# Second-tile ranks of the context dealt among its first tile's expert rows, and the context's experts dealt at three rates

## The chip, the cores and the metric

The kernel runs on one core of a Trainium2 chip. The metric is the device time of one execution in microseconds (us), the median of the runs shown. The program is one fixed order of instructions for each engine: PE (TensorE), DVE (VectorE), ACT (ScalarE), POOL (GpSimd) and SP (SyncE, which issues the loads of the weights). Engines wait for each other on semaphores alone.

## The reference, cut to what matters

256 tokens of width 1024, all in fp32, pass through a first model of two layers (a retention and state-space mixer, then a SwiGLU) and then through a second model of two layers (attention with a Fourier and a pooling branch, then a PEER layer that looks up 128 experts for each token). The second model also has a context of 256 tokens of its own, which nothing of the first model feeds: its modulation, its mixer and its PEER layer can be computed beside the first model.

```python
def _peer(h, w_pq, peer_keys, peer_down, peer_up):
    q = (h @ w_pq).reshape(B, L, PEER_HEADS, 2, PEER_QDIM // 2)
    s = jnp.einsum("blhpd,hpkd->blhpk", q, peer_keys)
    sv, si = lax.top_k(s, PEER_TOPK)                       # two top-16 of 128 for each of 8 heads
    cand = (sv[..., 0, :, None] + sv[..., 1, None, :])     # 256 sums
    top_s, pos = lax.top_k(cand, PEER_TOPK)                # the best 16, their experts' indices
    gate = jax.nn.softmax(top_s, axis=-1)
    a = jnp.einsum("tkd,td->tk", peer_down[ee], hh)        # one gathered row per expert
    act = gg * jax.nn.gelu(a)
    return jnp.einsum("tk,tkd->td", act, peer_up[ee])      # and a second one
```

## The kernel before, in words

A class `Plan` first writes one list of items (`put`), and five functions then turn the list into the engines' instructions, so an engine's order is the order of the items. Two generators write the items. The **main stream** (`x_stream`) is the first model and then the second model's two layers for the 256 tokens. The **context stream** (`context_stream`) is everything of the context. `streams` deals between them: each step of a generator says what it costs (`yield 7`; a step without a number costs 7), and the context is given its next step while its sum is at most the main stream's sum times a pace. The context changes the pace itself at three points: `PACES` is 0.8 in its modulation, 1.8 in its mixer, 1.1 in its queries and ranks, and 0.72 in its experts. When the first model is over (`yield "alone"`), what is left of the context is put at once; here the context ends a few items before that.

The first model's layer is, in this order: `conv_in` chunks, four groups of heads (`heads`, `group_gate`, `group_stats`, `group_turn`), a merge (`branch_gate`, `branch_out`), four retention heads, a second merge, the output product (`mix_out`, four products), a normalisation (`row_stats`, `row_turn`), 22 `ffn_in` products, 8 `ffn_out` and 2 `ffn_last`. Nearly every product is 32 PE records of one 1 MB weight chunk, about 7 us. After an `ffn_in` product DVE does two operations (L1966, L1968) that free the PSUM bank; four banks rotate, and `ffn_out` waits for the last L1968. In a group of heads PE waits for L1896, the decay factors that DVE makes.

The context's PEER layer is `peer_c`. For each of two tiles of 128 tokens and each of 8 heads a rank is made on DVE: `rank_keys` twice (L2130 to L2138, top 16 of 128), `rank_pairs` (L2149 and L2130 to L2138, top 16 of 256) and `rank_index` (L2157 to L2183, the experts' numbers). In the kernel before, `route` puts all 16 ranks, both tiles', before the first expert row. Then come 512 steps in the order (tile 0: 128 downs, 128 ups; tile 1: 128 downs, 128 ups), 1.5 of cost each. A step reads one row of 4 KB per partition, 0.52 MB in all, which POOL fetches by index (`fetch`, L2556) into a ring of nine places; a **down** (L2234) multiplies the row with the token's vector and sums, an **up** (L2245) adds the row times its activation to the result. A fetch of place i waits for the step that read the place before (`rows_read`), and the first nine wait for `gates_ok[1, 0]`, the gates of the second tile:

```python
rr = Ring([Slot(ar.get(1024), self.sem(f"row{i}")) for i in range(gslots)])
...
put("fetch", ..., before=s.before or gates_ok[1, 0])
```

The nine places lie where the queries, the keys and the scores were. `peer_add` closes the context: it loads a row into the first place and adds the result to the context. The main stream needs the context only in the second model.

Two merges, one in each layer, read DVE's L1954 and L1957; `mix_out` waits for the last of them.

## Time and profile before

| | before |
| --- | --- |
| median of 3 runs | 4141.52 us (4139.63 to 4145.15) |
| span of the profiled execution | 4145.5 us |
| PE busy | 3651.7 us, 88% |
| DVE busy | 2321.9 us, 56% |
| POOL busy | 1280.9 us, 31% |
| rows fetched by index | 855.71 MB, 51.5% of the 16 DMA engines' span |
| weights and the rest on SP's queue | 350.32 MB, 22.2% |

The profiled execution has no time of its own beside its span; the span lies within the range of the runs, 4.0 us above their median, and all sums are made against it. The first model fills about the first 2177 us, the second model the other 1969. "Busy" of PE counts the modelled time of its matmuls. The granted clock (PEclk) is a share of full speed; idle time is given before the group of instructions that ends it, with what it had waited for.

### The profile page before, as it was taken

The page shows a single profiled execution, that of the slowest core. Times are in us where ns is not written, and L with a number is a line of the kernel's source. Part 1 is how long each engine was busy: PE and PEld are TensorE (multiplying, and loading weights), DVE is VectorE, ACT ScalarE, POOL GpSimd, SP SyncE. Part 2 cuts the span into 40 slices and gives each one's busy share as a digit, 9 for nine tenths or more (in the row PEclk, how much of TensorE's full clock was granted, in tenths as well). Part 3 has the DMA queues.
Part 4 walks back from the last instruction along what each step waited for, and adds up shares of the span by engine and source line. Part 5 has one row for each costly group of instructions (what it writes and reads, how often), then busy time and mean ns, then how long its engine had stood idle before and what let it go on. Part 6 is the DMA issues. An engine that isn't in the chain of part 4 may idle for free. (4 is left out here: it accounts for less than half of the span.)

```text
span 4145.5 us, 41044 instructions
## 1 busy us (share of the span) xinstructions
PE 3651.7 (88%) x14584; PEld 2584.5 (62%) x14584; DVE 2321.9 (56%) x5464; ACT 657.1 (16%) x1800; POOL 1280.9 (31%) x1125
## 2 busy tenths in 40 slices
PE   8988999999989889999988989778788898877777
PEld 6666788887756778888846875333335686433332
DVE  3432011457676897775762137787763226777875
ACT  2332101110001230000002211111112211111111
POOL 1100000000664566664540003445441002444442
PEclk9999999999999899999999999999999999998899
DMA  8742344334998889998973349999996227999997
GB/s 324 283 194 88 117 151 180 134 111 145 369 411 292 295 330 395 405 389 340 413 298 125 108 152 384 415 416 401 419 415 256 103 107 288 404 420 420 418 420 331
DMA packets 207818, 1208.65 MB, mean 292 GB/s; under 512 B 23696, under 2 KB 24848, under 8 KB 96000
## 3 DMA queue, kind: packets, MB, share of 16 engines
q0 software_dynamic: 154368, 855.71, 51.5%
q1 hardware_dynamic: 53248, 350.32, 22.2%
q8 instruction: 118, 1.93, 0.2%
q14 instruction: 84, 0.69, 0.0%
HBM read 1204.79 MB, written 1.15 MB: 291 GB/s over the span
## 5 line engine op out<-in xcount | busy, mean ns | idle before, releaser
L1363 PE MATMUL bank<-big 128*128 128x256 f32 (+5 forms) x9848 | 2148.4, 378 | 59.5 <-issue 8.7
L1363 PEld LDWEIGHTS bank<-big 128*128 128x128 f32 (+2 forms) x9848 | 1839.0, 192 | 374.3 <-issue 67.4
L2556 POOL DMA_INDIRECT big<-in_pboth,big x1024 | 1217.5, 1189 | 1210.0 <-PE bank L1750 695.2
L1750 PE MATMUL bank<-big 128*128 128x512 f32 x2048 | 984.3, 638 | 251.2 <-ACT big L2520 251.0
L2234 DVE CUSTOM_DVE_ANT_0 big<-big 128x1024 f32<-128x1024 f32 x768 | 928.0, 1224 | 347.1 <-DMA big<-in_pboth,big 343.0
L1750 PEld LDWEIGHTS bank<-big 128*128 128x128 f32 x2048 | 407.5, 204 | 816.6 <-issue 481.4
L2543 POOL TENSOR_TENSOR big<-big 128x1 f32<-128x1 f32 (+1 forms) x49 | 37.4, 763 | 1499.4 <-DVE big L1804 1499.4
L2245 DVE SCALAR_TENSOR_TENSOR big<-big 128x1024 f32<-128x1024 f32 x254 | 326.2, 1284 | 61.3 <-DMA big<-in_pboth,big 41.5
L2520 ACT ACTIVATE big<-big 128x128 f32<-128x128 f32 x512 | 165.1, 391 | 254.9 <-DVE big L2213 248.2
L1398 PE MATMUL bank<-big 128*128 128x128 f32 x596 | 93.0, 290 | 63.5 <-ACT big L2365 20.1
L2510 ACT ACTIVATE big<-big 128x4 f32<-128x4 f32 (+2 forms) x134 | 27.7, 207 | 742.3 <-DVE big L2209 742.2
L1553 PE MATMUL bank<-big 128*128 128x512 f32 x256 | 114.5, 609 | 23.4 <-DVE big L1968 23.4
L2090 DVE TENSOR_REDUCE big<-bank 128x1 f32<-128x512 f32 (+1 forms) x48 | 28.9, 602 | 175.0 <-PE bank L1651 174.1
L1398 PEld LDWEIGHTS bank<-big 128*128 128x128 f32 x596 | 72.9, 151 | 80.8 <-issue 35.2
L1877 DVE SCALAR_TENSOR_TENSOR big<-big,bank 128x512 f32<-128x512 f32 x32 | 22.0, 687 | 148.8 <-ACT big L2346 148.8
L1553 PEld LDWEIGHTS bank<-big 128*128 128x128 f32 x256 | 49.8, 195 | 87.2 <-issue 63.1
L1954 DVE SCALAR_TENSOR_TENSOR big<-big,bank 128x256 f32<-128x256 f32 x32 | 13.4, 420 | 153.4 <-PE bank L1363 153.3
L1861 DVE SCALAR_TENSOR_TENSOR big<-bank,big 128x255 f32<-128x255 f32 (+1 forms) x144 | 62.7, 477 | 60.0 <-ACT big L2334 58.3
L2303 ACT ACTIVATE big<-big 128x1024 f32<-128x1024 f32 x26 | 27.4, 1056 | 428.4 <-DVE big L1974 170.8
L2112 DVE SCALAR_TENSOR_TENSOR big<-big,bank 128x512 f32<-128x512 f32 x36 | 24.8, 688 | 103.6 <-PE bank L1363 103.6
L2488 ACT ACTIVATE big<-bank,big 128x256 f32<-128x256 f32 x72 | 30.3, 472 | 282.1 <-PE bank L1363 282.1
L2549 POOL DMA_DIRECT2D big<-in_wmod x48 | 25.9, 542 | 150.9 <-PE bank L1575 150.9
(203 smaller groups left out, 2177.4 us busy)
## 6 DMA issues: line engine op xcount, KB each, us to landing
big<-in_w SPq DMA_DIRECT2D x104, 1024.0 KB, 7.7
big<-in_wmod POOLq DMA_DIRECT2D x48, 1024.0 KB, 9.0
big<-in_wgu SPq DMA_DIRECT2D x44, 1024.0 KB, 8.1
big<-in_wzg SPq DMA_DIRECT2D x36, 1024.0 KB, 4.8
big<-in_wro SPq DMA_DIRECT2D x32, 1024.0 KB, 6.9
big<-in_wpq SPq DMA_DIRECT2D x24, 1024.0 KB, 6.0
big<-in_wd SPq DMA_DIRECT2D x22, 1024.0 KB, 8.4
big<-in_pboth,big POOLq DMA_INDIRECT x1024, 11.7
```

What stands on the lines that cost most here:

```text
L1363: last = pe.matmul(o, a, b, start=(i == 0), stop=(i == n - 1))
L1398: last = pe.transpose(o[:, i, :], b, ident)
L1553: last = pe.matmul(us[2 * tt + n].ap, act[:, 2 * i + k, tt * P:tt * P + P], wk[:, k, 512 * n:512 * n + 512], start=(i + k == 0), stop=False)
L1750: last = pe.matmul(u.ap, d.ap, row[:, 512 * i:512 * i + 512], start=(k == 0), stop=(k == 127))
L1861: i = v.scalar_tensor_tensor(c[:, m, s:256], o[:, m, 0:256 - s], conv["w"][m][:, 3 - s:4 - s], c[:, m, s:256], ALU.mult, ALU.add)
L2090: step(v.reduce_max(sm[:, c:c + 1], u.ap[:, 0:nk * P], AX.X))
L2234: v.tensor_tensor_reduce(row, row, h, 1.0, 0.0, ALU.mult, ALU.add, out).then_inc(done[0], 1)
L2245: v.scalar_tensor_tensor(at, s.ap, by, at, ALU.mult, ALU.add).then_inc(done[0], 1)
L2488: last = e.activation(sc.ap[:, m, :], by2(u.ap)[:, m, :], ACT.Tanh, scale=0.5, bias=bias[m])
L2520: s.activation(d.ap, p.ident, ACT.Copy, scale=by).then_inc(diag[0], 1)
L2543: g.tensor_tensor(r.sm[:, 8 + r.at:8 + r.at + r.n], r.sm[:, 4 + r.at:4 + r.at + r.n], r.sm[:, 12:13].to_broadcast([P, r.n]), ALU.pow).then ...
L2556: g.indirect_dma_start(out=s.ap, out_offset=None, in_=table, in_offset=bass.IndirectOffsetOnAxis(ap=index, axis=0)).then_inc(s.full[0], 16)
```

## The change

Five things change, all in how the context is dealt.

1. `ranks` can be asked for one tile. `route` puts the first tile's 8 ranks only; the second tile's come one step at a time (`rank_keys`, `rank_keys`, `rank_pairs`, `rank_index`) before every third down of the first tile, steps 2, 5, 8 and so on to 101. The cost of those steps counts in the dealing as before.
2. The first downs therefore start when the first tile's gates are there (`gates_ok[0, 0]`).
3. The scores of the second tile and the scratch of the ranks must outlive the first downs. They move to the end of the context's memory (`kept`, 3248 columns), so only six places for rows fit at first; three more are placed at step 102, behind the second tile's gates (`gates_ok[1, 0]`). Places are no ring any more but a list of free ones, taken in the order in which they came free.
4. The pace of the experts is 0.9 instead of 0.72 until the main stream enters its second layer, 0.55 from there to that layer's first merge, and 0.75 after it. The main stream sets these two (`PACES[4]`, `PACES[5]`).
5. `peer_add` takes the first free place.

No operation is added or removed, on no engine: 32 `rank_keys`, 16 `rank_pairs`, 16 `rank_index`, 256 downs, 256 ups and 512 fetches in both. The items of the main stream keep their order. From line 1050 on lines are numbered up to 24 higher in the changed kernel; the down is L2258 there, the up L2269, the fetch L2580, L1954 and L1957 are L1978 and L1981.

```diff
--- before.py
+++ after.py
@@ -126,7 +126,7 @@
         self.before, self.ss, self.var, self.done = before, ss, var, done
 
 
-PACES = (0.8, 1.8, 1.1, 0.72)
+PACES = (0.8, 1.8, 1.1, 0.9, 0.55, 0.75)
 A_SIZE = 27648
 BIG_N = 53208
 SIDE = 8300
@@ -338,6 +338,8 @@
             yield 1.5
 
         for l in range(2):
+            if l:
+                yield "pace", PACES[4]
             blk = [0]
 
             def chunk(blk=blk, l=l):
@@ -571,6 +573,8 @@
                         yield 7.2 if first or n < 6 else 1
                     s.free(u.free)
 
+            if l:
+                yield "pace", PACES[5]
             yield from merge(True, y_ok, group_end(3, gots[3]))
             yield from head_qk(0, gots[4])
             for h in range(3):
@@ -1042,11 +1046,12 @@
         else:
             self.x_ok = done
 
-    def routing(self, ar, b2, wr, sm, l, vec, hT, hT_ok, keys, keys_ok, iot, iot_ok, tvs, gat, eix, qts, GH):
+    def routing(self, ar, b2, wr, sm, l, vec, hT, hT_ok, keys, keys_ok, iot, iot_ok, tvs, gat, eix, qts, GH, kept=None):
 
 
         put, tick, t = self.put, self.tick, self.t
         SC0 = Ring([Slot(ar.get(256, (2, 128))) for _ in range(3 if GH == 8 else 8)])
+        ar = kept or ar
         SC1 = ar.get(2048, (8, 256))
         rk = dict(cand=ar.get(256, (16, 16)), oh=ar.get(512, (32, 16)), sv=ar.get(32, (2, 16)), si=ar.get(32, (2, 16)),
                   sf=ar.get(32, (2, 16)), tp=ar.get(16).bitcast(U32), ab=ar.get(32, (2, 16)), ia=ar.get(32, (2, 16)),
@@ -1098,8 +1103,8 @@
             scores.append((sc, v.free))
             ended["keys"] = v.full
 
-        def ranks(asking=None):
-            for tt in range(2):
+        def ranks(asking=None, tiles=(0, 1)):
+            for tt in tiles:
                 for h in range(8):
                     while asking and len(scores) <= h:
                         next(asking)
@@ -1109,14 +1114,14 @@
                         yield from gates(tt, h // GH)
 
         def route():
-            first = rank_all = ranks()
+            first = ranks(tiles=(0,))
             for i in range(9):
                 if i < 8:
                     query(i)
                     yield 7
                     score(i)
                 for _ in range(4 if i else 0):
-                    yield next(rank_all)
+                    yield next(first)
             yield from first
 
         return route, query, score, ranks, ix_ok, gates_ok, ended
@@ -1146,32 +1151,51 @@
         got = yield from self.peer_queries(banks, sm, start, size, l, X, 1, self.c_ok, 2)
         ar, mark, h2, act, gat, eix, gl, hT, hT_ok, keys, rest = got
         m3 = ar.at
+        kept = Arena(self.big, start + size - 3248, 3248)
         rows = self.modulated_rows(l, 1, 3, "norm2", h2, [ar.get(1024) for _ in range(3)], self.b_free)
         rows_ok = yield from rows(hT_ok)
         ar.at = m3
         qts = Ring([Slot(ar.get(512, (2, 256)))])
         qts.slots[0].freed = rows_ok
-        tvs = [ar.get(128, (8, 16)) for _ in range(2)]
-        route, _, _, _, ix_ok, gates_ok, _ = self.routing(ar, banks, wr, sm, l, 1, hT, hT_ok, tvs=tvs, gat=gat, eix=eix, qts=qts,
-                                                       GH=8, **rest)
+        tvs = [kept.get(128, (8, 16)) for _ in range(2)]
+        route, _, _, ranks, ix_ok, gates_ok, _ = self.routing(ar, banks, wr, sm, l, 1, hT, hT_ok, tvs=tvs, gat=gat, eix=eix,
+                                                              qts=qts, GH=8, kept=kept, **rest)
         yield from route()
         yield "pace", PACES[3]
+        assert ar.at <= size - 3248
         ar.at = mark
-        rr = Ring([Slot(ar.get(1024), self.sem(f"row{i}")) for i in range(gslots)])
+        free = []
+
+        def place(ready):
+            s = Slot(ar.get(1024), self.sem(f"row{len(free) + len(ahead)}"))
+            s.freed = ready
+            free.append(s)
+
+        second = ranks(tiles=(1,))
         steps = [(kind, tt, k) for tt in range(2) for kind in range(2) for k in range(128)]
         pending, ahead, nxt, act_ok = [], [], 0, {}
         acc_ok = {}
+        while ar.at + 1024 <= size - 3248:
+            place(gates_ok[0, 0])
         for n, (kind, tt, k) in enumerate(steps):
-            while nxt < len(steps) and len(ahead) < gslots:
+            if n < 102 and n % 3 == 2:
+                yield next(second)
+            if n == 102:
+                assert next(second, None) is None
+                while len(free) + len(ahead) < gslots:
+                    place(gates_ok[1, 0])
+            while nxt < len(steps) and free:
                 kind2, tt2, k2 = steps[nxt]
-                s = rr.take()
+                slot = free.pop(0)
+                s = Turn(slot)
                 put("fetch", table=t["pboth"].rearrange("e (a d) -> (e a) d", a=2), s=s, index=eix[kind2][:, tt2, k2:k2 + 1],
-                    ready=ix_ok[tt2][k2 // 16] if k2 % 16 == 0 else None, before=s.before or gates_ok[1, 0])
-                ahead.append(s)
+                    ready=ix_ok[tt2][k2 // 16] if k2 % 16 == 0 else None, before=s.before)
+                ahead.append((s, slot))
                 nxt += 1
-            s = ahead.pop(0)
+            s, slot = ahead.pop(0)
             done = tick("rows_read")
             s.free(done)
+            free.append(slot)
             if kind == 0:
                 put("down", row=s.ap, full=s.full, h=h2[:, tt, :], out=act[:, tt, k:k + 1], done=done)
                 if k == 127:
@@ -1185,7 +1209,7 @@
                 acc_ok[tt] = done
             yield 1.5
         end = tick("peer_added")
-        put("peer_add", m5=rr.slots[0].ap, src=self.mods[l, 1, 5:6, :].to_broadcast([P, 1024]), loaded=tick("d_m5_c", 16),
+        put("peer_add", m5=free[0].ap, src=self.mods[l, 1, 5:6, :].to_broadcast([P, 1024]), loaded=tick("d_m5_c", 16),
             before=[done], acc=h2, X=X, done=end)
         self.c_ok, self.b_free = end, [end]
```

How DVE's order moves, at two places.

The end of the first layer's second merge, DVE, between two pairs L1954, L1957 of the merge (in the changed kernel L1978, L1981). Before, a pair and the first ten of the 29 rows that follow it up to the next pair:

```order
L1954 SCALAR_TENSOR_TENSOR big<-big,bank 128x256
L1957 TENSOR_TENSOR big<-big 128x256
L2130 MAX big<-big 128x8
L2132 MAX_INDEX big<-big 128x8
L2134 MATCH_REPLACE big<-big 128x128
L2136 MAX big<-big 128x8
L2138 MAX_INDEX big<-big 128x8
L2130 MAX big<-big 128x8
L2132 MAX_INDEX big<-big 128x8
L2134 MATCH_REPLACE big<-big 128x128
L2136 MAX big<-big 128x8
L2138 MAX_INDEX big<-big 128x8
```

The same place in the changed kernel:

```order
L1978 SCALAR_TENSOR_TENSOR big<-big,bank 128x256
L1981 TENSOR_TENSOR big<-big 128x256
L2258 ISA big<-big 128x1024
L2258 ISA big 128x1
L2173 TENSOR_TENSOR big<-big 128x256
L2154 MAX big<-big 128x8
L2156 MAX_INDEX big<-big 128x8
L2158 MATCH_REPLACE big<-big 128x256
L2160 MAX big<-big 128x8
L2162 MAX_INDEX big<-big 128x8
L2258 ISA big<-big 128x1024
L2258 ISA big 128x1
```

Before, a whole rank (two `rank_keys`, shown, then a `rank_pairs` and a `rank_index`) stands in this one gap. Now all that stands there is shown: two downs (an L2258 pair each) and one `rank_pairs`.

The second layer's groups of heads, DVE, one stretch from a group's mask (L1887) to the next group's first decay factor (L1895, L1896), where L2245 is the up. Before:

```order
L1887 TENSOR_TENSOR big<-bank,big 128x128
L2245 SCALAR_TENSOR_TENSOR big<-big 128x1024 x3
L1877 SCALAR_TENSOR_TENSOR big<-big,bank 128x2x256
L2245 SCALAR_TENSOR_TENSOR big<-big 128x1024 x2
L1906 TENSOR_TENSOR big<-big 128x512
L1908 TENSOR_TENSOR big<-big,bank 128x512
L1910 TENSOR_TENSOR big<-big 128x512
L1906 TENSOR_TENSOR big<-big 128x512
L1908 TENSOR_TENSOR big<-big,bank 128x512
L1910 TENSOR_TENSOR big<-big 128x512
L2245 SCALAR_TENSOR_TENSOR big<-big 128x1024 x2
L1895 SCALAR_TENSOR_TENSOR big<-big 128x256
```

In the changed kernel:

```order
L1911 TENSOR_TENSOR big<-bank,big 128x128
L2269 SCALAR_TENSOR_TENSOR big<-big 128x1024 x2
L1901 SCALAR_TENSOR_TENSOR big<-big,bank 128x2x256
L2269 SCALAR_TENSOR_TENSOR big<-big 128x1024 x3
L1930 TENSOR_TENSOR big<-big 128x512
L1932 TENSOR_TENSOR big<-big,bank 128x512
L1934 TENSOR_TENSOR big<-big 128x512
L1930 TENSOR_TENSOR big<-big 128x512
L1932 TENSOR_TENSOR big<-big,bank 128x512
L1934 TENSOR_TENSOR big<-big 128x512
L1919 SCALAR_TENSOR_TENSOR big<-big 128x256
```

Seven ups stood in this stretch and five do now; none is left in front of the next group's first decay factor.

The counts of context items by stretch of the main stream, as the two orders have them, are these; the prediction uses them.

| stretch of the main stream | before | changed |
| --- | --- | --- |
| between the last five products of the first layer's second merge | 6 keys, 3 pairs, 4 index | 10 downs, 2 keys, 1 pairs, 1 index |
| then to the last `row_turn` | 4 keys, 2 pairs, 1 index | 8 downs, 2 keys |
| then to the 22nd `ffn_in` | 71 downs, 4 keys, 2 pairs, 3 index | 65 downs, 10 keys, 6 pairs, 6 index |
| then to the second layer's first `row_turn` | 35 downs | 35 downs, 2 keys, 1 pairs, 1 index |
| then to the second layer's `dt_sums` (8 input products) | 22 downs, 15 ups | 9 downs, 23 ups |
| then to the last of its four groups of heads | 86 ups | 66 ups |
| then to the end of its second merge | 35 ups, 128 downs | 41 ups, 128 downs |
| then to the last `row_turn` | 7 ups | 8 ups |
| then to the 22nd `ffn_in` of the second layer | 84 ups | 87 ups |

## Rows read from the trace of the kernel before

**Rows 1.** The page's first line.
```profile
span 4145.5 us, 41044 instructions
```
**Rows 2.** Busy time by stretch; the first of them gives the columns.
```profile
core 0: us, PE busy (x) PEld busy (x) DVE busy (x) ACT busy (x) POOL busy (x), PEclk, DMA share, GB/s
...
1017.00:1194.00 177.00, 155.43 (x705) 134.71 (x706) 128.60 (x283) 8.57 (x23) 98.03 (x80) 0.95 0.90 354
...
1280.00:1361.00 81.00, 67.61 (x306) 58.01 (x306) 71.41 (x134) 12.55 (x27) 45.64 (x36) 0.90 0.87 313
1361.00:1567.00 206.00, 174.49 (x924) 154.32 (x924) 178.69 (x252) 67.86 (x191) 118.67 (x92) 0.92 0.85 315
1600.00:1896.00 296.00, 291.36 (x1333) 248.27 (x1332) 204.54 (x356) 19.59 (x43) 193.14 (x149) 0.99 1.01 399
1935.00:2099.00 164.00, 152.93 (x705) 133.21 (x705) 123.06 (x129) 8.47 (x22) 100.06 (x84) 0.98 0.99 397
...
2177.00:4146.00 1969.00, 1638.73 (x5237) 953.68 (x5235) 1136.37 (x3138) 351.22 (x1034) 582.82 (x529) 0.94 0.78 316
```
**Rows 3.** PE in order of time, end of the first layer's merge: start, length, idle before.
```profile
965.93 7.20 PE L1363 MATMUL bank<-big 128*128 128x256 f32 x32 [2.01 <-DVE big L1954]
978.50 30.09 PE L1363 MATMUL bank<-big 128*128 128x256 f32 x128 [5.37 <-issue]
...
1017.74 14.57 PE L1363 MATMUL bank<-big 128*128 128x256 f32 x66 [0.94 <-DVE big L1812]
```
**Rows 4.** PE in order of time, first layer's SwiGLU.
```profile
1054.28 126.83 PE L1363 MATMUL bank<-big 128*128 128x256 f32 x576 [8.54 <-DVE big L1968]
1193.40 21.79 PE L1553 MATMUL bank<-big 128*128 128x512 f32 x45 [12.29 <-DVE big L1968]
```
**Rows 5.** DVE in order of time, the context's last rank and its first down.
```profile
1031.89 0.30 DVE L2130 MAX8 big<-big 128x8 f32<-128x128 f32 x1
...
1033.74 0.29 DVE L2130 MAX8 big<-big 128x8 f32<-128x128 f32 x1
...
1042.37 0.29 DVE L2188 TENSOR_TENSOR big<-big 128x128 f32<-128x128 f32 x1
...
1052.20 1.23 DVE L2234 CUSTOM_DVE_ANT_0 big<-big 128x1024 f32<-128x1024 f32 x1 [8.10 <-DMA big<-in_pboth,big]
```
**Rows 6.** DVE by line, 1055 to 1194: count, busy us, mean ns, idle before.
```profile
L2234 DVE CUSTOM_DVE_ANT_0 big<-big 128x1024 f32<-128x1024 f32 x71 | 86.5, 1225 | 37.0 <-DMA big<-in_pboth,big 35.8
L1968 DVE TENSOR_TENSOR big<-big,bank 128x256 f32<-128x256 f32 x21 | 8.9, 422 | 0.7
```
**Rows 7.** The fetches L2556 from issue to landing, 1080 to 1190, saturated.
```profile
DMA to landing us min/median/max: 11.8/16.0/18.1
```
**Rows 8.** The same, 1350 to 1500.
```profile
DMA to landing us min/median/max: 4.9/6.5/9.7
```
**Rows 9.** POOL's time for one fetch, 1080 to 1190 and 2560 to 2700.
```profile
L2556 POOL DMA_INDIRECT big<-in_pboth,big x56: 935/974/1893, 1079.3 to 1189.1; - x56
...
L2556 POOL DMA_INDIRECT big<-in_pboth,big x55: 935/941/1791, 2560.6 to 2697.3; - x55
```
**Rows 10.** PE by line, second layer's groups of heads, 1361 to 1567.
```profile
L1484 PE MATMUL bank<-big 128*128 128x128 f32 x128 | 20.6, 311 | 6.0 <-DVE big L1849 6.0
...
L1474 PE MATMUL bank<-big 128*128 128x64 f32 x64 | 12.5, 279 | 13.0 <-DVE big L1896 13.0
L1398 PE MATMUL bank<-big 128*128 128x128 f32 x48 | 8.3, 301 | 14.6 <-ACT big L2365 14.6
```
**Rows 11.** DVE by line, the same stretch: the ups.
```profile
L2245 DVE SCALAR_TENSOR_TENSOR big<-big 128x1024 f32<-128x1024 f32 x89 | 114.3, 1284 | 7.7 <-issue 0.4
```
**Rows 12.** DVE by line, 1935 to 2099, second layer's SwiGLU: the ups.
```profile
L2245 DVE SCALAR_TENSOR_TENSOR big<-big 128x1024 f32<-128x1024 f32 x85 | 109.2, 1285 | 40.2 <-DMA big<-in_pboth,big 36.7
```
**Rows 13.** PE in order of time, the wait that ends that stretch.
```profile
2098.87 57.02 PE L1553 MATMUL bank<-big 128*128 128x512 f32 x128 [11.07 <-DVE big L1968]
```

## The prediction

> **What bounds the kernel now.** I start from the span [rows 1] and cut it by stage with the table of busy time [rows 2]. The last 1969 us are the second model; no item of it moves, so only the first 2177 us can change. There PE is what is waited for: nearly each product of 7 us follows the one before, and the time is PE's work plus the gaps in which it waits. So the question is which gaps the context's items cause, and I read PE in order of time for them. At the end of the first layer's merge there are gaps of 2.01 and 5.37 us [rows 3]: DVE is working off whole ranks, 10.5 us each (from the first MAX8 at 1031.89 to the gates at 1042.37) [rows 5], dealt at one per product of 7 us. In the first SwiGLU there are 8.54 and 12.29 us [rows 4]. The first of them is a chain: DVE finishes the last rank, only then may the first row be fetched, the down at the head of DVE's queue waits 8.10 us for it [rows 5], and PE's L1968 is behind that down. The second gap is DMA: from 1055 on the downs idle 37.0 us, 35.8 of them for their rows [rows 6]. In the second layer's groups of heads it is DVE itself: 178.7 of 206 us busy, PE only 174.5 [rows 2], with gaps of 13.0 us behind the decay factors, 14.6 behind ACT and 6.0 behind the step sizes [rows 10], while 89 ups take 114.3 us of DVE [rows 11]. The last gap is 11.07 us, before the second layer's `ffn_out` [rows 13]: again the ups idle 40.2 us, 36.7 of them for rows [rows 12], at a DMA share of 0.99 [rows 2].
>
> A gap also costs PE speed. The four output products behind the 5.37 us gap take 30.09 us for 128 records, 0.235 us each; behind the 8.54 us gap 576 records take 126.83 us, 0.220 each [rows 3, 4]. 128 × 0.015 is 1.9 us lost to the lower granted clock, which stands at 0.95 in the SwiGLU, at 0.92 in the heads and at 0.99 in the stretch with hardly a gap [rows 2].
>
> **Term 1, the merge of the first layer.** Between its last five products DVE had 6 keys, 3 pairs and 4 index steps. A key step is 1.85 us (1031.89 to 1033.74), a whole rank 10.5 [rows 5], so this is some 34 us over some 28 us of PE. Now it is 10 downs and one step of each other kind. A down is 1.225 us [rows 6] and the read of its sum behind it, 1.28 from start to start: 10 × 1.28 + 10.5 = 23 us. DVE keeps up, and of 2.01 + 5.37 us there is left what the last pair of operations needs, under 2. With the 1.9 us of clock the gain is **8 us**. What could take the place: the first row is asked for when the first gates are done and holds DVE up, by at most the 8.1 us of [rows 5]; but that is four products earlier, and 28 − 23 us of slack and a bank's depth lie between.
>
> **Term 2, the first SwiGLU.** The last `row_turn` now ends at 1017.7 − 8 = 1009.7 [rows 3]. From there to the 22nd L1968 DVE has 65 downs (65 × 1.28 = 83.2), six ranks less two key steps (6 × 10.5 − 2 × 1.85 = 59.3) and 22 pairs of 0.42 us [rows 6] with a handover (22 × 0.86 = 18.9), in all 161.4 us. PE needs 22 × 32 × 0.220 = 155. So DVE, not DMA, sets this stage now. To it I add waits for rows. The bounds are 0 and the 37.0 us of [rows 6]. Six places instead of nine speak for more, but the rows needed fall from 71 to 65 over a stretch that saturated DMA with 71, and steps of ranks between the downs give the fetches time. Fetches below saturation land in 6.5 us, in saturation in 16.0 [rows 7, 8]; with issue and down a place turns round in 6.5 + 2.2 = 9 us at best, and six of them are wanted each 6 × 161/65 = 15 us. I take 4 us, near the good end. `ffn_out` then starts at 1009.7 + 161.4 + 4 = 1175 instead of 1193.4: **18 us with term 1**. PE still waits some 10 us there, now for DVE.
>
> The Trainium skill speaks against this very interleaving. First the row: a fetch takes POOL 974 ns at the median where only downs run, and 941 ns in a stretch of the second model in which ranks run beside the fetches, each with four casts and five scalar operations [rows 9]. By the page "SBUF — State Buffer", section "Who interferes with whom", a copy, cast or tensor_scalar in a two-port mode shuts GpSimd out of their shared port pair, and with it the writing of descriptors for DMAs issued by POOL. By that rule each rank could add up to the length of its casts to a fetch; by the row it adds nothing, and the sum goes by the row.
>
> **Term 3, `ffn_out` to the second layer's `dt_sums`.** 35 downs stand in `ffn_out` and `ffn_last` in both, four rank steps (10.5 us) come on top, in a stage where PE asks DVE for nothing: hidden, if DVE is not behind by more than its last 20 us. Then 22 downs and 15 ups (22 × 1.28 + 15 × 1.3 = 48 us) become 9 and 23 (41 us). PE idles 81 − 67.6 = 13 us here [rows 2], for DVE. But nine of the downs stand in front of the very first input product. **5 us** gain, between 0 and 8.
>
> **Term 4, the heads.** 86 ups become 66: 20 × 1.3 = 26 us of DVE go (1.284 each [rows 11]). Of the 33.6 us of gaps [rows 10] the 6.0 is behind a queue that gets one up shorter, the 13.0 is behind ups put in front of the decay factors, the 14.6 behind ACT, which waits for DVE further up. DVE falls to 153 of 206 us, PE's 174 then lead. Bounds: 0, if the chain DVE, ACT, PE in a group costs the same however short the queue; 26, all of DVE's relief; 33.6 and some clock is a limit it cannot pass. I take a bit over half: **15 us**.
>
> **Term 5, what was put off.** At the end of the heads 12 experts are missing from the count (20 fewer ups there, 8 more before). They come back where DMA is saturated: 6 more rows in the second merge stage (share 1.01, 399 GB/s [rows 2]) one behind it and 3 more in the second SwiGLU (0.99); the last two come after that. A row of 0.524 MB is 1.31 us at 399 GB/s. In the first of these PE idles only 296 − 291.4 = 4.6 us, with nine rows in hand; of 6 × 1.31 = 8 us of DMA I let 2 through. In the second the wait for DMA is already open [rows 13], and all of 3 × 1.31 = 4 adds to the 11.07. **6 us loss**, between 1 and 12. `peer_add` moves behind the main stream's first `ffn_add`, where DVE waits for PE; nothing. Queue order on POOL: the roots of the normalisations now have fetches before them in the first layer too; each fetch waits for an earlier down only, so at most one issue of 0.94 us each, nothing.
>
> **The sum:** −18 − 5 − 15 + 6 = −32 us against a span of 4145.5, so 4113. The median of the runs lies 4.0 below the profiled span: 4141.5 − 32 = 4109.5, I say **4109**.
>
> **The rivals.**
> - *Heads give nearly everything, and more clock.* Terms 3 and 4 at their good ends, 8 + 26, no waits in term 2 (4) and 3 in term 5: some −50, **4091**. For it: PE loses speed behind each gap. Against: a group's own chain stays. 0.15.
> - *The put-off rows come back in full.* Term 5 at 12, and term 4 at 6, because ACT's share of the gaps stays: −18 − 5 − 6 + 12 = −17, **4124**. For it: share 1.01 in the stage that gets more. 0.17.
> - *The dealing moves the gaps without closing them*, so the change doesn't do what it says: DVE-bound first SwiGLU with 15 more us of waits, heads at 6, term 5 at 12: about **4139**. 0.10.
> - *Six places are too few: slower.* Place: the downs up to step 102, in the first SwiGLU. If fetches land there as in saturation, 16.0 to 18.1 us [rows 7], a place turns in about 18 to 20 us, a row comes each 3.0 to 3.4 us, and the 65 rows need 195 to 220 us instead of 161, that is 34 to 59 us of waits instead of 4. It is slower than before from 36 us on, a turn of some 18.2 us; between 36 and 59 us, at 48, the total is **4153**. For it: the ring shrinks by a third while the pace rises. Against: fewer rows ask DMA for less, and landing falls as soon as it is not saturated [rows 8]. 0.08.
>
> **How the numbers follow.** The forecast has 0.50 (its own range 4096 to 4122), the rivals 0.15, 0.17, 0.10 and 0.08. The range leaves out the fast rival's outer half, most of the slow one and half of the unmoved one: 4086 to 4138. Within 0.2% (8.3 us, about what a measurement of this kernel can tell from none) is 4133.2 to 4149.8. Faster by more: 0.50 + 0.15 + 0.17 less a bit for the tails, 0.80; same 0.12; slower 0.08.
>
> **What would show it.** Right: the first down at about 940, no wait of 8 us at DVE for it; the gap before `mix_out` under 2 us; no gap at the fifth `ffn_in`; a gap of about 10 us before the first `ffn_out`, at about 1175, with DVE busy over 0.9 in that stage and its DMA share under 0.9; the gaps of the heads near half of 33.6; the gap before the second `ffn_out` at about 15. Wrong: downs that idle more than 15 us for rows in the first SwiGLU (the six places), heads with gaps above 28 us (a chain, no queue), or gaps for rows in the second merge stage, where there are none now.

## The result, and the profile after

| | before | changed |
| --- | --- | --- |
| median | 4143.34 us (4 runs) | 4096.9 us (4 runs, 4094.54 to 4104.84) |
| ratio of the runs, changed to before | | 0.9894, 95% interval 0.9882 to 0.9906 |
| span of the profiled execution | 4145.5 us | 4095.9 us |

The change makes the kernel 1.06% faster, 46 us between the medians, where 32 were forecast. In a later comparison on another occasion it came to 0.9891 (0.9875 to 0.9908).

The busy time by stretch in the changed kernel, columns as in [rows 2], each stretch cut at the same products of the main stream as there:

```profile
1006.00:1162.00 156.00, 153.53 (x706) 133.53 (x707) 145.95 (x389) 8.45 (x22) 76.88 (x65) 1.00 0.94 359
...
1246.00:1321.00 75.00, 64.92 (x306) 55.33 (x306) 66.16 (x116) 12.31 (x27) 40.59 (x31) 0.95 0.85 306
1321.00:1511.00 190.00, 170.01 (x925) 150.20 (x926) 154.26 (x233) 68.65 (x193) 95.77 (x73) 0.96 0.80 287
1544.00:1842.00 298.00, 290.07 (x1325) 246.96 (x1324) 213.75 (x362) 19.55 (x42) 197.03 (x155) 0.99 1.01 404
1880.00:2051.00 171.00, 153.38 (x705) 133.56 (x706) 129.03 (x134) 8.45 (x22) 113.80 (x87) 0.96 0.99 397
...
2129.00:4096.00 1967.00, 1644.83 (x5236) 954.81 (x5234) 1135.04 (x3137) 350.83 (x1034) 580.68 (x529) 0.94 0.78 316
```

The first SwiGLU went from 177 to 156 us, the input products and heads from 81 + 206 to 75 + 190, and the second SwiGLU from 164 to 171. The table below has the same from the start of one product of the main stream to the start of another; the last two columns compare it with the terms of the prediction.

| stretch of the main stream | before | changed | difference | forecast |
| --- | --- | --- | --- | --- |
| start to the first layer's fourth retention head, 882 (order unchanged) | 881.9 | 877.9 | −4.0 | 0 |
| to the first `ffn_in` (term 1) | 135.8 | 128.9 | −6.9 | −8 |
| to the first `ffn_out` (term 2) | 175.7 | 154.5 | −21.2 | −10 |
| to `dt_sums` (term 3) | 160.5 | 154.7 | −5.8 | −5 |
| to the second layer's first merge product (term 4) | 224.5 | 204.5 | −20.0 | −15 |
| to its first `ffn_in` (term 5) | 356.6 | 360.3 | +3.7 | +2 |
| to its first `ffn_out` (term 5) | 163.9 | 169.6 | +5.7 | +4 |
| to the end | 2046.6 | 2045.5 | −1.1 | 0 |

PE in order of time, at the places of [rows 3, 4] and [rows 13]:

```profile
968.01 27.97 PE L1387 MATMUL bank<-big 128*128 128x256 f32 x128 [1.12 <-issue]
...
1161.27 19.16 PE L1577 MATMUL bank<-big 128*128 128x512 f32 x44 [1.64 <-DVE big L1992]
...
2050.43 9.80 PE L1577 MATMUL bank<-big 128*128 128x512 f32 x18 [16.81 <-DVE big L1992]
```

The 5.37 us before `mix_out` are 1.12, and the four products behind it take 27.97 us instead of 30.09: that is the clock, granted at 1.00 over these four products where it was 0.93 before, with the lower level at their start, behind the gap. The gap of 8.54 us is gone, that of 12.29 is 1.64, and the last one grew from 11.07 to 16.81. DVE by line in the first SwiGLU, against [rows 6], and the fetches' landing there:

```profile
L2258 DVE CUSTOM_DVE_ANT_0 big<-big 128x1024 f32<-128x1024 f32 x66 | 77.9, 1217 | 0.1
L1992 DVE TENSOR_TENSOR big<-big,bank 128x256 f32<-128x256 f32 x22 | 9.3, 422 | 0.8
L1990 DVE SCALAR_TENSOR_TENSOR big<-big,bank 128x256 f32<-128x256 f32 x22 | 9.2, 418 | 5.1 <-ACT big L2429 5.0
```
```profile
DMA to landing us min/median/max: 5.0/8.6/10.4
```

The downs idle 0.1 us instead of 37.0; DVE even waits 5 us for ACT. The rows land in 8.6 us instead of 16.0 [rows 7], with ranks between the downs and with six places instead of nine; how much of it the places alone do is seen below, in the run with six places throughout. The price I had wrong is in the same kernel, DVE in order of time:

```profile
1010.67 1.21 DVE L2258 CUSTOM_DVE_ANT_0 big<-big 128x1024 f32<-128x1024 f32 x1
1011.80 0.08 DVE L2258 DVE_READ_ACCUMULATOR2_ANT big<- 128x1 f32 x1
1011.80 1.22 DVE L2258 CUSTOM_DVE_ANT_0 big<-big 128x1024 f32<-128x1024 f32 x1
```

From one down to the next it is 1.13 us, not 1.28. In the kernel before, every pair of downs at 1.28 us has a wait for the row in it, 0.04 or 0.05 us in the trace, and the few pairs without such a wait follow each other at 1.14 to 1.15 there too.

The heads, PE by line, against [rows 10]:

```profile
L1508 PE MATMUL bank<-big 128*128 128x128 f32 x128 | 18.7, 292 | 3.8 <-DVE big L1873 3.8
...
L1498 PE MATMUL bank<-big 128*128 128x64 f32 x64 | 12.0, 269 | 5.0 <-DVE big L1920 5.0
L1422 PE MATMUL bank<-big 128*128 128x128 f32 x49 | 8.6, 300 | 14.7 <-ACT big L2389 11.8 <-ACT big L2344 2.9
```

33.6 us of gaps are 23.5, of which 2.9 belong to a turn that stands outside the stretch of [rows 10]. 13.0 behind the decay factors became 5.0. PE's own time in these stretches fell as well, from 174.5 to 170.0 us, at a granted clock of 0.96 instead of 0.92.

### The profile page after: what moved, and what is told of

The parts are those of the page before. It is cut to its first block and busy times, and to the rows that moved or that the text cites. A ratio compares the mean times of both kernels' runs of the same rounds, so it can differ in the third digit from the quotient of the medians.

```text
span 4095.9 us, 41049 instructions
## 1 busy us (share of the span) xinstructions
PE 3641.8 (89%) x14584; PEld 2573.2 (63%) x14584; DVE 2316.0 (57%) x5464; ACT 656.3 (16%) x1800; POOL 1283.3 (31%) x1125
## 3 DMA queue, kind: packets, MB, share of 16 engines
HBM read 1204.79 MB, written 1.15 MB: 294 GB/s over the span
## 5 line engine op out<-in xcount | busy, mean ns | idle before, releaser
L2580 POOL DMA_INDIRECT big<-in_pboth,big x1024 | 1217.8, 1189 | 1277.7 <-PE bank L1774 700.4
L2258 DVE CUSTOM_DVE_ANT_0 big<-big 128x1024 f32<-128x1024 f32 x768 | 926.0, 1222 | 317.7 <-DMA big<-in_pboth,big 314.0
L2269 DVE SCALAR_TENSOR_TENSOR big<-big 128x1024 f32<-128x1024 f32 x254 | 326.2, 1284 | 65.8 <-DMA big<-in_pboth,big 45.4
L1978 DVE SCALAR_TENSOR_TENSOR big<-big,bank 128x256 f32<-128x256 f32 x32 | 13.5, 421 | 147.8 <-PE bank L1387 147.8
L2327 ACT ACTIVATE big<-big 128x1024 f32<-128x1024 f32 x26 | 27.4, 1055 | 363.7 <-DVE big L1998 128.2
```

What stands on the lines that cost most here:

```text
L2258: v.tensor_tensor_reduce(row, row, h, 1.0, 0.0, ALU.mult, ALU.add, out).then_inc(done[0], 1)
L2269: v.scalar_tensor_tensor(at, s.ap, by, at, ALU.mult, ALU.add).then_inc(done[0], 1)
L2580: g.indirect_dma_start(out=s.ap, out_offset=None, in_=table, in_offset=bass.IndirectOffsetOnAxis(ap=index, axis=0)).then_inc(s.full[0], 16)
```

## The experiments

Theory A is that of the prediction: the order of the ranks closes the first layer's gaps, the low pace those of the heads, and rows put off are paid for where DMA is saturated. All are made from the changed kernel, except where it is said, and all twelve keep the main stream's order. Stage times are from the profiled executions, in the table's sense.

### The order alone, the paces alone

```diff
-PACES = (0.8, 1.8, 1.1, 0.9, 0.55, 0.75)
+PACES = (0.8, 1.8, 1.1, 0.72, 0.72, 0.72)
```

> The changed kernel with its experts at 0.72 throughout, so only the order of the second tile's ranks and the six and then nine places are new. Theory A (the order closes the first layer's gaps, the low pace the heads' gaps, and what is put off costs about 9 us): the first layer keeps nearly all of its 32 us, the heads' 18 and the input products' 8 are lost, the 9 us of put-off rows are not paid: about 4115 us, gap before the second ffn_out near 11 us. Theory B (the three paces do it, the order only permits them): the gap before the first ffn_out is 8 us or more again and the total 4130 or above.

Measured: 4140.42 us, ratio 0.9998 (0.9987 to 1.0008). Neither number was met, but the stages tell why. The first layer keeps its gain: 154.6 us from its first `ffn_in` to the first `ffn_out`, where the changed kernel has 154.5, with a gap of 1.76 us. The heads take 222.8 us again (86 ups), the second SwiGLU 163.2. What had not been in the expectation is the end. The rank steps now cost their share of 0.72 beside the rows, so ten rows are left when the first model is over; they are put at once, and the second model's first product waits. PE in order of time:

```profile
2181.53 1.94 PE L1422 MATMUL bank<-big 128*128 128x128 f32 x8 [28.57 <-DVE big L2061]
```

So the order is worth its 28 us in the first layer at the old and at the new paces, and at the old pace the second model gives 27 back, because the context isn't finished.

The kernel before with the new paces (its list of ranks and its ring as they were):

```diff
-PACES = (0.8, 1.8, 1.1, 0.72)
+PACES = (0.8, 1.8, 1.1, 0.9, 0.55, 0.75)
...
+            if l:
+                yield "pace", PACES[4]
...
+            if l:
+                yield "pace", PACES[5]
```

> The kernel before, all ranks ahead of the first row and nine places at once, with the three new paces (0.9, 0.55, 0.75). Theory A: the first row's wait of 8 us stays, and at 0.9 the downs ask for 4.2 rows and a weight chunk in each 7 us, above what DMA gave (414 GB/s), so the gap before the first ffn_out grows to 20 us or more; the heads gain some 18, the end loses a few: 4135 to 4150 us. Theory B (the paces do it): 4110 or less.

Measured: 4158.79 us, ratio 1.0032 (1.0021 to 1.0044): the paces without the order are slower than the kernel before. The first SwiGLU takes 197.5 us (36.8 + 160.7) instead of 175.7; the heads take 203.1, as with the new order. DVE by line and the stretch itself, 1052 to 1211:

```profile
L2238 DVE CUSTOM_DVE_ANT_0 big<-big 128x1024 f32<-128x1024 f32 x87 | 104.8, 1224 | 39.0 <-DMA big<-in_pboth,big 38.2
```
```profile
1052.00:1211.00 159.00, 130.37 (x575) 110.79 (x573) 119.28 (x216) 7.34 (x19) 109.04 (x89) 0.93 1.02 409
```

89 rows at 409 GB/s: DMA is full. What the order gives the first SwiGLU is therefore that 59 us of DVE work on ranks lies there and takes the place of rows, beside the row that no longer has to be waited for. That the rows are fewer (65 instead of 89) is counted; how the gain divides between the two is not.

### The heads: how much an up costs

```diff
-PACES = (0.8, 1.8, 1.1, 0.9, 0.55, 0.75)
+PACES = (0.8, 1.8, 1.1, 0.9, 0.75, 0.75)
```

> The changed kernel with 0.75 instead of 0.55 in the second layer's heads. Theory A (gaps in the heads are DVE's queue of ups): the heads take 18 to 22 us longer, the context ends earlier, and the gap before the second ffn_out is no longer than 17 us: about 4112. Theory C (the gaps there are the chain DVE, ACT, PE of a group and the gain came from the clock and the input products): under 8 us longer, about 4100.

Measured: 4140.65 us, ratio 0.9997 (0.9987 to 1.0007). More than I expected: this one number gives back nearly all the change had won. 26.5 us are the heads (231.0 with 90 ups against 204.5 with 66) and 8.6 the input products (78.2 against 69.6; 40 rows against 32); from the second merge to the SwiGLU it is 6.9 us more, the SwiGLU itself 3.4 more. The SwiGLU's part has another cause: the context ends inside it, the gap before `ffn_out` is only 2.00 us, and one product before it PE waits for a weight chunk instead. The section on moving rows shows why. PE in order of time:

```profile
2085.12 9.88 PE L1387 MATMUL bank<-big 128*128 128x256 f32 x32 [15.23 <-DMA big<-in_wgu]
```

PE by line in the heads:

```profile
L1508 PE MATMUL bank<-big 128*128 128x128 f32 x128 | 21.5, 320 | 6.6 <-DVE big L1873 6.6
...
L1498 PE MATMUL bank<-big 128*128 128x64 f32 x64 | 13.3, 292 | 14.7 <-DVE big L1920 14.7
L1422 PE MATMUL bank<-big 128*128 128x128 f32 x48 | 8.4, 302 | 13.2 <-ACT big L2389 13.2
```

The ends of the gaps are the same engines as in the changed kernel; what changed with the number of ups is how long they last, and the time of a matmul (320 ns against 292 in the first row): the clock stood at 0.90 there and at 0.96 in the changed kernel. What an up costs here is therefore DVE's time and the clock together.

```diff
-PACES = (0.8, 1.8, 1.1, 0.9, 0.55, 0.75)
+PACES = (0.8, 1.8, 1.1, 0.9, 0.35, 0.75)
```

> The changed kernel with 0.35 in the second layer's heads: 42 ups instead of 66 in the groups of heads and 23 instead of 32 rows in the input products; 23 rows are left for the end of the first model. From the runs so far an up in the heads costs about 1.0 us (86, 66 ups: 224.5, 204.5 us from dt_sums to the second merge's first branch_out). Theory A (DVE's queue all the way): about 182 us. Theory C (a group's own chain takes over once the queue is short): 195 us or more. The rows left over cost at least 30 us at the start of the second model, so the total is 4105 to 4130 either way.

Measured: 4125.32 us, ratio 0.9962 (0.9948 to 0.9976). From `dt_sums` to the merge 184.8 us with 42 ups. The points are 231.0, 204.5 and 184.8 us at 90, 66 and 42 ups, with 222.8 at 86 in the changed order at the old pace and 224.5 at 86 in the kernel before: 0.9 to 1.0 us for an up between 86 and 66, some 2 above 86, 0.8 below 66. Theory A holds nearly all the way, and the chain begins to show; PE by line:

```profile
L1508 PE MATMUL bank<-big 128*128 128x128 f32 x128 | 17.8, 282 | 0.4 <-DVE big L1873 0.4
...
L1498 PE MATMUL bank<-big 128*128 128x64 f32 x64 | 11.5, 261 | 0.0
L1422 PE MATMUL bank<-big 128*128 128x128 f32 x60 | 10.1, 296 | 10.2 <-ACT big L2389 8.7 <-ACT big L2344 1.5
```

Nothing is left behind the decay factors; 8.7 us behind ACT are still there. Whether fewer ups would shorten those too was not run. The total is lost at the end, where 23 rows were left over, and one wait is 46.99 us:

```profile
2160.54 1.94 PE L1422 MATMUL bank<-big 128*128 128x128 f32 x8 [46.99 <-DVE big L2061]
```

### The end: rows left over

```diff
-PACES = (0.8, 1.8, 1.1, 0.9, 0.55, 0.75)
+PACES = (0.8, 1.8, 1.1, 0.9, 0.55, 0.72)
```

> The changed kernel with 0.72 instead of 0.75 from the second layer's first merge on; some nine rows are left for the end of the first model and are put there at once. Theory A (the put-off rows cost DMA time in the saturated stage, one row 1.3 us): the gap before the second ffn_out falls from 16.8 to 11 to 13 us, total 4090 to 4096, if the rows at the end hide beside ffn_last and the first products of the second model. Rival: the rows at the end hold the second model's first rows up by 9 x 1.3 us, total 4100 or more.

Measured: 4104.17 us, ratio 0.9904 (0.9888 to 0.9921). The total is the rival's, and both mechanisms are there: the gap before the second `ffn_out` is 9.69 us, shorter than theory A's 11 to 13 (83 rows instead of 87, the stage 7.1 us shorter), and 17.31 us of gap stand at the start of the second model. Only two rows were left by the order, not nine; but ups put off stood before them, and `peer_add` behind them. DVE in order of time, the last of the context and the main stream's next operation:

```profile
2127.84 9.80 DVE L2269 SCALAR_TENSOR_TENSOR big<-big 128x1024 f32<-128x1024 f32 x7
2142.11 2.36 DVE L2288 TENSOR_TENSOR big<-big 128x1024 f32<-128x1024 f32 x2 [4.46 <-DMA big<-mods]
2144.50 2.36 DVE L2291 TENSOR_TENSOR big<-big 128x1024 f32<-128x1024 f32 x2
...
2147.72 0.75 DVE L2061 TENSOR_SCALAR big<-big 128x1024 f32<-128x1024 f32 x1 [0.67 <-POOL big L2567]
```

Seven ups (9.8 us), a load that is asked for only when the last up is done (4.5) and the four operations of `peer_add` (4.7) stand in DVE's queue before L2061. Whether one row or ten is left, this tail is paid: 17 us for two, 29 for ten, 47 for 23, that is 1.4 us for each further row, which is what an up takes behind another. The paces of the changed kernel end the context one product before the end of the first model, and pay none of it. The prediction had no term for this tail.

### The places

```diff
-        while ar.at + 1024 <= size - 3248:
+        while len(free) < 4:
             place(gates_ok[0, 0])
```

> The changed kernel with four places for rows instead of six until step 102 (then nine, as before). Theory A (in the first SwiGLU DVE's own work sets the stage, a place turns round in landing 8.6 us and 2.2 us more, 11 us, and is wanted again after as many rows as there are places, 2.4 us each): four places give one row per 2.7 us, some 0.3 us too slow, so the stage from the first ffn_in to the first ffn_out grows by 10 to 20 us from 154.5 and the total is 4105 to 4117. Rival (places have slack, landing shortens with the load): under 3 us longer, total below 4100.

Measured: 4127.13 us, ratio 0.9961 (0.9947 to 0.9976). The total is above the expected 4105 to 4117. The first SwiGLU takes 173.2 us instead of 154.5 (+18.7), within the 10 to 20 expected; the downs idle 20.5 us for rows although these land in 7.1:

```profile
L2258 DVE CUSTOM_DVE_ANT_0 big<-big 128x1024 f32<-128x1024 f32 x55 | 66.0, 1220 | 20.5 <-DMA big<-in_pboth,big 20.4
```

Another 6 us are lost before it, from the fourth retention head to the first `ffn_in` (135.0 against 128.9): the gap before `mix_out` is 5.29 us again. With six places the list has slack, with four it is what the stage waits for.

```diff
-        yield from self.peer_c(self.pb, Ring(few), self.smallb, self.B0 + mark, BIG_N - self.B0 - mark, 9, 0, self.C)
+        yield from self.peer_c(self.pb, Ring(few), self.smallb, self.B0 + mark, BIG_N - self.B0 - mark, 6, 0, self.C)
```

> The changed kernel with six places for rows to the end instead of nine from step 102 on. Theory A (places matter only while they turn round slower than rows are wanted; in saturation landing was 16 us with nine places because nine stood in DMA's queue, and with six it shortens): the saturated stages of the second layer take at most 10 us longer, total 4097 to 4107. Rival (landing stays at 16 us, a place turns in 18, six give a row per 3 us where one per 2.1 is wanted): the second SwiGLU alone grows by 40 us or more, total 4140 or above.

Measured: 4125.0 us, ratio 0.9959 (0.9944 to 0.9973), 26 us behind the changed kernel on the same occasion (4098.74): between the two expectations. The mechanism is A's, the size is not. In the second SwiGLU the fetches land in 9.5 us instead of 15.9:

```profile
DMA to landing us min/median/max: 4.8/9.5/12.6
```

so a place does turn faster when fewer are in the queue, and that stage loses 3.0 us. But in the stages before it 5.1 us go in the input products, 2.2 + 8.3 in the second merge and retention heads and 5.6 in its end, 4.4 of them in the gap before `mix_out`. In the merge stage DVE idles 69.8 us for rows, where it is 15.3 in the changed kernel; DVE by line, 1525 to 1870:

```profile
L2258 DVE CUSTOM_DVE_ANT_0 big<-big 128x1024 f32<-128x1024 f32 x128 | 154.5, 1226 | 61.3 <-DMA big<-in_pboth,big 60.5
L2269 DVE SCALAR_TENSOR_TENSOR big<-big 128x1024 f32<-128x1024 f32 x32 | 41.1, 1285 | 11.9 <-DMA big<-in_pboth,big 9.3 <-DVE big L2269 0.5
```

Nine rows in hand bridge most of that. The three places that come back at step 102 are worth 22 us in the profiled executions, about as much as the relief of the heads.

### Can rows be moved out of the saturated stage?

Two kernels put other paces into the second layer's `ffn_in` and `ffn_out`: 0.68 and 0.95, and 0.66 and 1.05.

```diff
-PACES = (0.8, 1.8, 1.1, 0.9, 0.55, 0.75)
+PACES = (0.8, 1.8, 1.1, 0.9, 0.55, 0.75, 0.95, 0.68)
...
+            if l:
+                yield "pace", PACES[7]
             fr = Ring([wa[2], wt[0], wt[1], wa[0], wa[1]])
...
+            if l:
+                yield "pace", PACES[6]
             us = [wide.take() for _ in range(4)]
```

> The changed kernel with 0.68 instead of 0.75 in the second layer's ffn_in and 0.95 in its ffn_out: 80 rows instead of 87 in front of the first ffn_out, 38 instead of 31 behind it, and the context ends one product earlier. Theory A (a row in the DMA-saturated ffn_in costs 1.3 to 1.9 us, one in ffn_out nothing, since PE needs nothing of DVE there): ffn_in to ffn_out falls from 169.6 to 157 to 160 us, total 4083 to 4089. Rival (the rows in ffn_out hold DVE beyond ffn_add and give it back): 4095 or more.

> The same with 0.66 and 1.05: 78 rows and 40. Theory A: ffn_in stage 155 to 158 us, near PE's own 153; 40 rows and 11 weight chunks are 32 MB, in 77 us just what DMA gave (414 GB/s), so up to 3 us may come back at ffn_last: total 4081 to 4089. Rival: 4095 or more.

> The changed kernel itself, on the same chip as the other three, to compare them with: 4093 to 4101 by every theory.

Measured: 4096.59 us (ratio to before 0.9894, 0.9877 to 0.991), 4095.85 (0.9886, 0.9869 to 0.9902), and the changed kernel beside them 4098.74 (0.9891, 0.9875 to 0.9908). No difference that can be told. Half of theory A is right: from `ffn_in` to `ffn_out` it is 156.1 and 154.7 us instead of 168.7, 1.8 and 1.6 us for each row. The other half did not come. PE in order of time in the kernel with 0.68:

```profile
2035.06 56.97 PE L1581 MATMUL bank<-big 128*128 128x512 f32 x128 [3.32 <-DVE big L1996]
2102.37 2.93 PE L1591 MATMUL bank<-big 128*128 128x512 f32 x3 [10.34 <-DMA big<-in_wd]
```

Behind the eight `ffn_out` PE waits 10.34 us (11.53 in the other) for the weights of `ffn_last`. The chunks are not slow, they are asked for late. They land a median 8.6 us after they are issued, 8.3 in the changed kernel. SP issues them behind `peer_add`'s load, which waits for the context's last up. SP's queue, its issues in order of time and the wait before the first:

```profile
2095.41 0.33 SPq L2655 DMA_DIRECT2D big<-mods  x1
2095.78 1.56 SPq L2602 DMA_DIRECT2D big<-in_wd  x3
```
```profile
SPq L2655 <- DVE big L2273: 37.4, 1, 37.4
```

SP stands still for 37.4 us (38.6 in the other) with the three chunks of `ffn_last` behind that load, and asks for them 0.4 us after it. In the changed kernel the last chunks of `in_wd` are issued by 2093.8 us, and `peer_add`'s load comes at 2103.0, behind them. In the kernel before SP stands too, for 21.8 us, but asks for the three chunks at 2144.0 us, 11.7 before `ffn_last` starts, and PE waits for none of them. In the run with 0.75 in the heads it is the same with the last `ffn_in` chunk: SP waits 42.5 us for the last up, issues the load at 2078.13 and the chunk at 2078.50, and PE waits 15.23 us. So the runs do not show that rows in `ffn_out` cost anything by themselves; what cost the 10 us is the place of the context's last load in SP's queue. An estimate from these rows is that the two kernels would be some 10 us faster with that load put behind the weights; it was not run.

### Starting the rows earlier

```diff
-PACES = (0.8, 1.8, 1.1, 0.9, 0.55, 0.75)
+PACES = (0.8, 1.8, 1.8, 0.85, 0.45, 0.72)
```

> The changed kernel with the context's queries and ranks at 1.8 instead of 1.1, so that its rows start some 60 units of the main stream earlier, and the rows then at 0.85, 0.45 and 0.72. Theory A: the heads have 55 ups instead of 66 (11 us less) and 27 instead of 32 in the input products (3 to 5 us less), the gap before the second ffn_out is 11 instead of 16.8 us, and the first layer pays at most 4 us for ranks in its retention heads: about 4080. Rival (the earlier ranks delay DVE in the first layer's heads and merge by as much as is won): about 4097.

Measured: 4116.23 us, ratio 0.9939 (0.9922 to 0.9956). The second layer gained what was expected (heads 194.5 us, second SwiGLU 160.6), but the first layer's first `mix_out` starts at 1004.5 instead of 968.0. The largest gap on the way:

```profile
912.43 2.05 PE L1537 MATMUL bank<-big 128*128 128x512 f32 x2 [11.44 <-DVE big L1960]
```

This is a retention head's product of scores and values. DVE's mask of the scores (L1960) stands behind seven downs and two steps of ranks, and the first of these downs waits for the first row:

```profile
899.22 1.23 DVE L2258 CUSTOM_DVE_ANT_0 big<-big 128x1024 f32<-128x1024 f32 x1 [7.34 <-DMA big<-in_pboth,big]
```

In the changed kernel the same first row, waited for 5.4 us, falls into the merge, where PE has a bank in hand. The mixer at 2.4 as well was worse:

> As the run with the early ranks, and the context's mixer at 2.4 instead of 1.8, rows at 0.85, 0.45 and 0.70: rows start some 110 units earlier than in the changed kernel, and the last stage asks for 81 rows instead of 87. Theory A: 4070 to 4080, the gap before the second ffn_out below 10 us. Rival (a denser mixer makes PE wait for ACT and DVE in the first layer's heads by more than that): above 4085.

Measured: 4136.8 us, ratio 0.9986 (0.9976 to 0.9996); the first `mix_out` starts at 1022.6, and the second SwiGLU, with 81 rows, takes 158.3. Its first SwiGLU is slower too, 161.0 us with 72 rows in it. Up to `mix_out` the changed kernel takes 968.0 us with PE busy 900.6, these two 1004.5 with 915.2 and 1022.6 with 921.0, for the same 4520 records: 22 and 34 us are more idle time, 15 and 20 are PE's own time at a granted clock of 0.96 and 0.95 instead of 0.98. Which of the gaps each early step makes was not taken apart.

## Why the prediction was right, and where it was off

The measured 4096.9 us lies in the range of 4086 to 4138, on the side that was forecast, 12 us below the forecast of 4109. The terms sum to −32, the profiled executions show −44.5 in the stretches the change touches and −5 in the two it doesn't touch, which is within what runs of one kernel differ.

- **Term 1** (−8, measured −6.9) was right with its mechanism: DVE keeps up, 1.12 us of gap stay, and the clock's 2 us are in the four products' own time.
- **Term 2** is the term that was mis-sized, −10 where −21.2 was measured. The reading that DMA no longer sets this stage was right, and so was the number of operations. The step that DVE sets it instead was not: PE does, with one run of 152.8 us and a gap of 1.64, while DVE waits 5 us for ACT. Two prices were wrong in the same direction. I took 1.28 us for a down from start to start, from a stretch in which each down waited a little for its row; where the rows are in hand it is 1.13 to 1.15, 65 × 0.14 = 9 us less. And I added 4 us of waits for rows, where there are 0.1. Without both, my own sum for the stage is 152 us, below PE's 153 or so, and the forecast 10 us of gap is the 1.64 of the trace. One sign failed with it: the DMA share of the stage is 0.94, not under 0.9; that DMA sets nothing there is shown by the downs' 0.1 us, not by the share.
- **Term 3** (−5, measured −5.8) was right in size. The runs with 40 and 23 rows there (78.2 and 64.7 us against 69.6) bear out that it is the number of rows.
- **Term 4** (−15, measured −20.0) was in its bounds. The gaps gave about what was forecast: 8.0 us behind the decay factors, 2.2 behind the step sizes, 2.8 behind ACT, and 1.4 at the turn that ends the heads, 14.4 in all. What the term left out is PE's own time, 4.5 us less at the higher clock; the prediction named the clock only as part of a limit.
- **Term 5** (+6, measured +9.4) was right in kind. Its two parts were 3.7 and 5.7. I priced a row at 1.31 us in the second SwiGLU; from 78 rows to 87 (154.7, 156.1, 162.5, 163.9, 169.6 us at 78, 80, 83, 84, 87) it is some 1.7 us a row. Why it is more than the row's transfer is open. In the stage before, DVE idles 15.3 us for rows where it idled 6.9, and PE waits 4.76 us before the fourth retention head's product where it waited 2.80.
- The **slower rival** (six places too few) was not what happened with six places, and its mechanism was shown with four: +18.7 us in that stage. The **rival of rows coming back in full** was not what happened either: 9.4, not 12, and the heads gave more, not less. With 0.75 in the heads, though, the kernel is as slow as before, so the forecast held for these paces and not for any.
- **The port.** In the changed kernel, with six ranks beside 63 fetches, POOL takes 946 ns for a fetch at the median, where it took 974 before [rows 9]: no lengthening is seen, as the sum had it. A median can't tell a few lengthened fetches, and it moves for other reasons: beside ups alone it is 940 in the kernel before (1950 to 2090) and 1116 in the changed one (1890 to 2045). What is shown is that it costs nothing here, since the downs idle 0.1 us. By the Trainium skill, page "SBUF — State Buffer", section "Who interferes with whom", the casts could have lengthened a fetch; the trace shows no lengthening of the median.
- **What the prediction overlooked** is that the old pace would not have finished the context. It priced each stage and not the tail behind the last one, where two rows left over cost 17 us. It also put the new place of `peer_add` at nothing. That came true, but by where these paces happen to end the context: its load stands behind SP's last chunk of `in_wd`, and its last operation before the second model. In three runs that load came ahead of weights and PE waited for them (15.23, 10.34 and 11.53 us), in three others the second model waited for the rows left over. The sum had neither, so this nothing was luck.

## What to carry to other kernels

When work of one stream is dealt among another's, price a unit of it per stage by the resource that is full there, here DVE in the heads (about 1.0 us a row), DMA in the second SwiGLU (about 1.7). Then look at the queue that issues the loads: rows moved to `ffn_out` kept no product waiting for DVE, but a load that waits for the context's last row stood ahead of weights in SP's queue and held them up. The first unit of a stream that waits for a transfer belongs where the other engine has a buffer in hand, and the last must end before the point that waits for the whole stream, with its load not in front of weights that are needed sooner. Take the price of an operation from trace rows in which it is in the state that the change will put it in, not from rows in which it waits.

## What the runs showed of the hardware

- A down, a custom DVE operation with a read of its sum, is 1.13 to 1.15 us from start to start where its rows have long landed. Where DMA is saturated 1.28 is the commonest, with a wait of 0.04 or 0.05 us for the row in it. Its busy time is 1.22 in both, so it starts before the one ahead has ended when nothing holds it.
- An up is busy 1.28 us. Each adds to the result of the one before, and they follow at 1.41 to 1.43; the operation of the main stream behind the last of them starts 1.20 after it. By these two times, 20 fewer ups in the heads are an estimated 27 us of DVE, where the prediction had 26.
- A fetch of 0.52 MB landed in 6.5 us at some 300 GB/s, in 16 at 410 GB/s with nine places, and in 9.5 at 398 GB/s with six: with DMA nearly full in both, it is the number of fetches outstanding that differs.
- SP issues its loads in order, and a load that waits for another engine holds up all behind it: SP stood for 37.4 us, and the next chunk was issued 0.4 us after the load that had waited.
